# Attention scores of two heads in pairs: the third mixer's score matmuls in two PSUM banks, without a wait between the halves

## The reference, cut to what matters

```
q, k, v, xr, yr = split(rms_norm(x) @ w_in)
q = axial_rope(rms_norm(q)) * 64 ** -0.5        # 8 heads
k = axial_rope(rms_norm(k))                     # 2 heads, each serves 4 query heads
p = softmax(q k^T)                              # per head, in blocks of 128 queries, 256 keys
attn_out = p v
xc = conv4(xr)
lru_out = (rg_lru(xc, forward) + rg_lru(xc, backward)) * gelu(yr)
x = x + concat(attn_out, lru_out) @ w_out
```

## Time and profile before

| | us |
|---|---|
| median of 3 runs | 2225.24 |
| lowest, highest | 2222.77, 2225.49 |
| profiled execution, its time | 2221.32 |
| its span (first to last instruction) | 2219.5 |
| TensorE busy in the span | 2133.1 |
| third mixer's attention, first score to last exponential | 1932.92 to 1963.3 |
| the stage's end, where the output projection's main part starts | 1982.21 |

### The profile page before, as it was taken

The page is one execution under the profiler, slowest core; times in us unless marked ns, Lnnn a source line. Parts: engine busy times, 40 slices in busy tenths (PEclk is TensorE's granted clock), DMA queues, the critical chain, the costliest instruction groups (busy, mean ns, idle before and its releaser), DMA issues.

```text
span 2219.5 us, 26215 instructions
## 1 busy us (share of the span) xinstructions
PE 2133.1 (96%) x10706; PEld 1726.3 (78%) x10706; DVE 1524.6 (69%) x1811; ACT 1098.8 (50%) x1102; POOL 58.0 (3%) x64
## 2 busy tenths in 40 slices
PE   8989999998898999999999999999999999999998
PEld 7578688884785887878788787888778786758997
DVE  4675644456756888888898886544588888546766
ACT  1232344221321776767677774434367674545554
POOL 0220000002100000000000000000000000100000
PEclk9999999999998999999999999999999999999999
DMA  8202454531023898989899895555579996316460
GB/s 318 76 1 77 181 196 143 201 115 63 1 77 135 304 373 324 372 322 367 327 366 370 323 377 206 184 182 194 185 289 365 327 369 223 114 39 237 163 227 20
DMA packets 209150, 484.44 MB, mean 218 GB/s; under 512 B 9200, under 2 KB 15088, under 8 KB 208112
## 3 DMA queue, kind: packets, MB, share of 16 engines
q1 hardware_dynamic: 209008, 482.50, 60.1%
HBM read 481.44 MB, written 1.05 MB: 217 GB/s over the span
## 4 chain that ended last, share of the span: by engine, by line
PE 84%; DVE 9%; ACT 4%; issue 2%; POOL 1%; DMA 0%; DVEq 0%; ACTq 0%; SPq 0%; POOLq 0%
PE bank L967 20%; PE bank L969 20%; PE bank L968 20%; PE bank L596 11%; PE bank L799 4%; PE bank L603 2%; PE bank L760 1%; DVE e_lo L1844 1%; DVE b_X L1366 1%; ACT e_hi L2249 1%; DVE b_arena L1360 1%; DVE b_XT L1360 1%; DVE b_arena L1366 1%; PE bank L1237 1%; DVE b_arena L1363 1%
## 5 line engine op out<-in xcount | busy, mean ns | idle before, releaser
L1844 DVE TENSOR_TENSOR e_lo<-b_ring,e_hi 128x2048 fp32r<-128x2048 f32 (+1 forms) x407 | 925.0, 2281 | 336.5 <-ACT e_hi L2249 334.0
L2249 ACT ACTIVATE e_hi<-b_ring 128x2048 fp32r<-128x2048 f32 (+1 forms) x407 | 776.7, 1911 | 306.8 <-PE bank L969 302.5
L967 PE MATMUL bank<-e_hi,e_xh 128*128 128x512 f32 (+1 forms) x1200 | 471.8, 393 | 19.7 <-DVE e_lo L1844 10.2
L969 PE MATMUL bank<-e_hi,e_xl 128*128 128x512 f32 (+1 forms) x1200 | 466.0, 388 | 0.0
L968 PE MATMUL bank<-e_lo,e_xh 128*128 128x512 f32 (+1 forms) x1200 | 465.5, 388 | 0.0
L967 PEld LDWEIGHTS bank<-e_hi,e_xh 128*128 128x128 f32 x1200 | 226.6, 189 | 67.4 <-issue 22.0
L967 PE MATMUL bank<-e_hi,e_th 128*128 128x512 f32 x688 | 269.2, 391 | 0.4 <-DVE e_tl L1848 0.4
L968 PE MATMUL bank<-e_lo,e_th 128*128 128x512 f32 x688 | 267.9, 389 | 0.0
L969 PE MATMUL bank<-e_hi,e_tl 128*128 128x512 f32 x688 | 267.7, 389 | 0.0
L969 PEld LDWEIGHTS bank<-e_hi,e_xl 128*128 128x128 f32 x1200 | 226.3, 189 | 47.1
L968 PEld LDWEIGHTS bank<-e_lo,e_xh 128*128 128x128 f32 x1200 | 226.8, 189 | 44.2
(11 more groups left out here) (237 smaller groups left out, 2212.5 us busy)
## 6 DMA issues: line engine op xcount, KB each, us to landing
b_ring<-in_moe_w SPq DMA_DIRECT2D x168, 2048.0 KB, 9.9
b_ring<-in_ffn_w SPq DMA_DIRECT2D x15, 2048.0 KB, 8.3
b_ring<-in_w_in SPq DMA_DIRECT2D x14, 2048.0 KB, 9.7
b_ring<-in_w_up SPq DMA_DIRECT2D x12, 2048.0 KB, 8.0
b_ring<-in_w_down SPq DMA_DIRECT2D x6, 2048.0 KB, 8.7
b_ring<-in_w_o SPq DMA_DIRECT2D x4, 2048.0 KB, 7.9
b_gain<-in_gains SPq DMA_DIRECT2D x6, 1024.0 KB, 4.9
b_ring<-in_w_out SPq DMA_DIRECT2D x2, 2048.0 KB, 7.8
```

What stands on the lines that cost most here:

```text
L967: e.matmul(out, ah, bh, start=first, stop=False)
L969: return e.matmul(out, al, bh, start=False, stop=last)
L1844: e.tensor_tensor(lo, raw, r32(hi), ALU.subtract).then_inc(lo_dve.sem)
L2249: return e.activation(out, x, ACT.Copy)
```

## The change

TensorE takes two banks at once for a head pair, one for the upper and one for the lower half of the array, and writes both query blocks into them: four matmuls in a row without a wait. A bank is given back when the exponentials of the second tile (n = 2h + 1) are done. The scores of a pair go at i = 0, 2, 4, 6, one tile earlier than before for odd tiles. VectorE reduces each bank to the maxima of one half for both tiles (two reductions), and negates all four at once, signalling two tiles. ScalarE reads a tile's two halves from two banks. The gate matmuls stay at i = 2, 3, 5.

```diff
-            att2_order += [("score", i)] * (i < 8) + [("turn", i - 2)] * (2 <= i < 10) + [("out", i - 3)] * (i >= 3)
+            if i < 8 and i % 2 == 0:
+                att2_order += [("score", i // 2, m) for m in range(2)]
+            att2_order += [("turn", i - 2)] * (2 <= i < 10) + [("out", i - 3)] * (i >= 3)
...
-                def scores(n):
-                    h, t = n // 2, n % 2
-                    b = B.take()
-                    for m in range(2):
-                        p = 64 * m
-                        if m:
-                            e.wait_ge(*score2(0, 2 * n))
-                        e.matmul(bank[b][:, 256 * m:256 * m + 256], qT2[p:p + 64, h, tok(t)], kT2[p:p + 64, h // 2, :],
-                                 start=True, stop=True).then_inc(score2.sem)
-                    B.until(b, s2_exp(0, n))
+                def scores(h):
+                    both = [B.take() for _ in range(2)]
+                    for t in range(2):
+                        for m, b in enumerate(both):
+                            p = 64 * m
+                            e.matmul(bank[b][:, 256 * t:256 * t + 256], qT2[p:p + 64, h, tok(t)], kT2[p:p + 64, h // 2, :],
+                                     start=True, stop=True).then_inc(score2.sem)
+                    for b in both:
+                        B.until(b, s2_exp(0, 2 * h + 1))
...
-                    s8 = sm2[:, n % 4, :]
-                    e.wait_ge(*score2(0, 2 * n + 1))
-                    ch(e.tensor_reduce(s8[:, 0:2], bank[att2_bank["score", n]][:, :].rearrange("p (m k) -> p m k", m=2), AX, ALU.max))
+                    s8 = sm2[:, 2 * h % 4:2 * h % 4 + 2, :]
+                    for m in range(2):
+                        e.wait_ge(*score2(0, 4 * h + 2 + m))
+                        ch(e.tensor_reduce(s8[:, :, m:m + 1], view(bank[att2_bank["score", h, m]][:, :], 2, 256), AX, ALU.max))
                     ch.wait()
-                    ts(s8[:, 2:4], s8[:, 0:2], -1.0, None, ALU.mult).then_inc(s2_max.sem)
+                    ts(s8[:, :, 2:4], s8[:, :, 0:2], -1.0, None, ALU.mult).then_inc(s2_max.sem, 2)
```

More of the change, by code:

```diff
@@ L1272, in third_attention @@
                 for i in range(11):
[L1273 to L1276, removed]
+                    if i < 8 and i % 2 == 0:
+                        scores(i // 2)
+                    if i in (2, 3, 5):
+                        next(gates, None)
                     if 2 <= i < 10:
@@ L2174, in third_attention @@
                 for i in range(11):
-                    if i < 8:
-                        scores(i)
+                    if i < 8 and i % 2 == 0:
+                        scores(i // 2)
                     yield
@@ L2616, in scores @@
                 def scores(n):
-                    e2, s8, b = E2[:, n % 3, :], sm2[:, n % 4, :], bank[att2_bank["score", n]]
+                    e2, s8, t = E2[:, n % 3, :], sm2[:, n % 4, :], n % 2
                     e.wait_ge(*s2_max(0, n))
@@ L2621, in scores @@
                     for m in range(2):
-                        ins = e.activation(e2[:, 256 * m:256 * m + 256], b[:, 256 * m:256 * m + 256], ACT.Exp,
+                        b = bank[att2_bank["score", n // 2, m]]
+                        ins = e.activation(e2[:, 256 * m:256 * m + 256], b[:, 256 * t:256 * t + 256], ACT.Exp,
                                            bias=s8[:, 2 + m:3 + m], scale=1.0, accum_out=s8[:, 4 + m:5 + m])
```

## The result

| | before | after |
|---|---|---|
| median, us | 2223.63 (20 runs) | 2228.19 (20 runs) |
| lowest to highest | 2217.95 to 2227.18 | 2225.39 to 2232.08 |
| ratio | | 1.0021, 95% interval 1.0014 to 1.0028 |
| span of the profiled execution | 2219.5 | 2228.3 |

The kernel is 4.6 us slower, 0.2%, and neither interval reaches down to 1: in a second set (experiment e1) the ratio is 1.0013, interval 1.0004 to 1.0022, or 2.9 us. The time itself is the forecast 2228.1, but partly by luck: the forecast added 2.9 us to a median of three runs, 2225.24, and the median of twenty is 1.6 lower.

What follows compares the result with a forecast made beforehand. TensorE, busy for 96% of the span, bounds the kernel, and the start of tile 5's transposes decides the stage. The middle of B and C, +2.9 us, on the median 2225.24 gave 2228.1 us, range 2223 to 2231.

Steps and rivals of the forecast that it cites:

- Step 1: Score matmuls on TensorE: all 16 take 4.2 us instead of 10 at full clock; the first eight about 1.8 us.
- Step 2: First exponential on ScalarE: two VectorE reductions now precede it, so it comes 0.69 us later.
- Step 3: Third exponential (tile 2) on ScalarE: its reductions start later and it comes 1.35 us later.
- Step 4: First products with the values: their bank waits for exponential 3, so +2.25 us, with a TensorE stall of about 4.9.
- Step 5: After the first long stall, half clock to the gates' end: transposes of tile 3 come 0.56 us later.
- rival A: Clock stays high over the first stall, or is high again by the second score group: -1.5 us; chance 0.12.
- Step 6: Transposes of tile 5: their bank waits for exponential 7, not 6, so +2.07 us, with a stall of about 3.5.
- Step 7: Dense tail behind the second long stall: a lowered clock there costs between 0 and 3.5 us.
- B: Clock low up to the gates' end, with no fall in the tail: +2.1 us; chance 0.25.
- C: As B, with 3.4 us of low clock in the tail: +3.8 us; chance 0.27.
- the bound of 0.2%: Whole kernel: a measurable difference, 4.45 us; chance 0.20 on the slow side, 0.05 on the fast side.

Runs made afterwards that it cites:

- e1: The changed kernel run again without any edit, for the scatter; ratio to the kernel before 1.0013 (1.0004 to 1.0022).
- e2: The changed kernel with the third attention's banks from a list over six instead of four in turn; ratio to the kernel before 0.9995 (0.9986 to 1.0005).
- e3: The changed kernel with idle matmuls filling its three TensorE stalls; ratio to the kernel before 0.9988 (0.9977 to 0.9998), stage 47.48 us.
- e6: The changed kernel with three idle matmuls in the last long stall alone; ratio to the kernel before 1.0013 (1.0003 to 1.0022).
- e4: The kernel before with two idle matmuls in its stall ahead of the first products; ratio to the kernel before 0.9986 (0.9977 to 0.9995), stage 44.63 us.
- e8: The changed kernel with six banks and five idle matmuls in the first long stall; ratio to the kernel before 0.9968 (0.9957 to 0.9979).
- e7: The kernel before with a tile's halves in two banks from six, no wait between them, no pairing; ratio to it 1.0005 (0.9997 to 1.0014).

## Why the prediction was right, step by step

**Step 1, the scores.** Eight matmuls in 1.93 us (1.8 forecast). TensorE did have the time back, in front of a wait.

**Step 2.** Exponential 0 stands 3.65 us behind the first score instead of 2.97: +0.68, forecast +0.69.

**Step 3.** Exponential 2: 10.85 instead of 9.53, +1.32, forecast +1.35.

**Step 4.** First products: 13.32 instead of 11.18, +2.14, forecast +2.25; the stall is 4.87, forecast 4.9. e2 shows what released it: in a bank that no later pair has used it comes at 12.50.

**Step 5.** t3 was to be 0.56 later. The first profile has it 0.82 earlier, two others 0.53 and 0.63 later than the repeated before (23.16 and 23.26 against 22.63). The step assumed half clock up to the gates' end. In the first profile the clock came back inside the gates, which took 2.31 us (1956.91 to 1959.22) and not 3.51. At full clock a third bank wait shows, as rival A had it: 0.90 us ahead of t3 in e3.

**Step 6.** From t3 to t5 7.42 us, forecast 7.52, with a stall of 3.48, forecast 3.5. The mechanism is right. The start of t5 itself was to be 2.07 later; it is 0.59 later in the first profile, and 1.6 and 1.7 in the two others against the repeated before. What the step did not see is how much of the wait a freer bank saves: t5 can come 3.8 us behind t3 (e2), since most of the wait is for table loads and the gate's activation, which the bank rotation of before had put ahead of it as well.

**Step 7.** 0 to 3.5 us in the tail; it was 2.43, 1.31 and 1.36. The step charged a whole stretch at half clock to the tail; part of each lay in the stall in front, so the 6.8 us of the first profile cost 2.4 and not 3.4.

The Trainium skill, "TensorE: Matmul & The Clock Gate", section "Why this matters for your kernels", which was weighed here, is borne out for both long stalls, in each profile of the changed kernel, and not for the short one: a wait of 2.04 us was followed by half clock in all three profiles of before. The 3.33 us at 1612.56 passed without it.

**The sum** was +2.9 for the stage; it is +3.0 in the first profile, and +3.0 and +3.1 for the two others against the repeated before. In size that is better than its parts deserve. In the first profile they are t5 +0.6 and tail +2.4 where the forecast, the middle of B and C, had 2.07 and 0.85: two errors of 1.5 us that cancel, by luck. In the two others they are +1.6 or 1.7 and +1.3 or 1.4, between B and C in the tail, and errors of 0.4 to 0.5 cancel. And e3 is rival A made real: 1.8 us below before, 1.5 forecast. The time in the first set has moved 4.6 us. The 1.5 us behind the stage were in no step; with them that set comes to the bound of 0.2%, which had been given one chance in five. That the forecast time of 2228.1 was met all the same is the luck named at the start: these 1.5 us and a baseline that was 1.6 too high cancel.

## What to carry to other kernels

When a group takes two tiles' worth of a bank, look up which signal gives the bank back, and who takes it next; a matmul that is ready on its data can wait for a later tile, and for everything that stands ahead of that tile on its engine. A faster group in front of a wait only lengthens the wait, so a saving there is worth nothing until the wait's own releaser is earlier; and a longer wait on TensorE can bring half clock behind it. Compare two orders at full clock first (idle matmuls in the stalls do it): the difference then is the order's own.

## What the runs showed of the hardware

- The clock: after the wait of 2.04 us it was half for 10.2 us in three of three profiles of before. The wait of 1.71 us in the changed kernel was followed by none, that of 4.87 by 10.2 us in three of three profiles (6.8 in e6), that of 3.48 by 6.8, 3.4 and 3.4 us. After one of 3.33 us elsewhere none followed. After the same wait of 1.90 us, at 2011.28 and its like, it fell in three of three profiles of the changed kernel and in none of three of the kernel before. Idle matmuls in the waits held it at 1.00 over the stage in e3, e4 and e8.
- In f32, four matmuls that contract over 64 partitions, alternating between the two halves of the array and two banks, take 1.06 us with the change of shape; two without a wait take 0.64 (e7), two with a wait between them 1.38.
- Two reductions ahead of the first exponential put it 1.60 us behind their start, one 0.92. A version in which ScalarE starts on the first tile while VectorE still reduces the second was not run, so what it would do is not shown.
